# A mixer in another order: the decay chain ahead of the recurrent inputs, four of six gate projections among later products

## The chip, the cores and the metric

The kernel runs on one core of a Trainium2 chip, in one launch. The metric is the device time of that launch in microseconds. Three runs of the kernel before gave 1144.72, 1143.68 and 1144.16, a median of 1144.16. All times below are in microseconds (us) unless marked otherwise. TensorE (PE) multiplies matrices, VectorE (DVE) and ScalarE (ACT) do the elementwise work, GpSimd (POOL) does some, and SyncE (SP) issues most transfers.

## The reference

One layer of a hybrid decoder, in float32, over 256 prompt rows, 16 meta rows and 8 x 4 sample rows, 1024 wide. A layer norm, a mixer of three parallel branches behind one input projection and one output projection, a residual with layer norm, and a mixture of 32 experts, four for each row, with a layer norm behind it.

```python
# mixer, from the reference (cut)
xa, ga, vb, gb, q, k, v, rc, z = split(x @ w_in)
xc = conv4(xa)                       # branch a: recurrence
y_a = rglru(xc, ...) * gelu(ga)      # sigmoid gates from xc, a linear scan over time
uc = conv31(vb * sigmoid(gb))        # branch b: long convolution
y_b = silu(layer_norm(uc))
g = log_sigmoid(z @ w_gate2 + b_gate) / 16
o = gated_linear_attention(q, k, v, cumsum(g))   # branch c
y_c = rms_norm(o) * silu(rc)
y = concat(y_a, y_b, y_c) @ w_out
h = layer_norm(alpha * x + y)
out = layer_norm(alpha * h + moe(h))
```

The states of the three branches (the last inputs of both convolutions, the last hidden vector, the attention's matrix) are outputs too.

## The kernel before

The kernel is written engine by engine. Each engine has one list of instructions in a fixed order, and semaphores hold an instruction until what it needs is there. No scheduler changes this order.

TensorE's work in the mixer is a list of jobs (`JOBS`), one for each result in PSUM. A job writes bank (number of the job modulo 8), and it must wait until the job eight places earlier has been read out of that bank. The order of `JOBS` is thus both TensorE's order and the assignment of banks. `filled(eng, job)` waits until the job is in its bank, `copied(eng, job)` until it has been read.

The names of jobs: V0 to V2 values, VB and GB the long convolution's inputs and gates, XA0 to XA2 the recurrent inputs, K, Q and G keys, queries and decays, RG and IG the recurrence's two block gates (three each), GA0 to GA2 the gate projections of branch a, R0 to R2 those of branch c. KT and SC are transposed keys and scores of a chunk (0, 1 for the prompt, 2 for the samples), O outputs, STM and ST states, MU and VAR mean and variance of branch b, OA and OB state columns for output, W00 to W11 states of the samples, YC transposed outputs of branch c. P2 and P00 to P11 are the output projection, H and LG its normalised rows and the router's logits, POS the routing.

What the prediction's steps touch, with lines of the kernel before:

- The decay chain: G is added a bias (DVE L1048), ScalarE takes the softplus (L702 to L706), VectorE scans (L1053), ScalarE takes exponentials (L731 to L741), VectorE multiplies queries and keys (L1077 to L1092). The scores (L1544) wait for `qk_decayed`.
- The recurrence: short convolutions of XA on VectorE (L997 to L1001), RG and IG (PE L1433), their sigmoids (ACT L716), tanh and exponentials (L748, L751), products (DVE L1095 to L1102), a root (ACT L753) and the scan (DVE L1109). Its result times the Gelu of GA is `ya` (L1175).
- The long convolution: 31 taps for each of two parts on VectorE (L978 to L987). Their calls `taps(m, k0, k1)` are spread among the other work.
- The residual rows: the first layer norm's rows times gain and plus shift (DVE L1028, L1032), needed by the layer norm behind the mixer.
- The late part: MU, the square (ACT L802), VAR, a root, the reciprocal (DVE L1215), Silu (ACT L815); P2 (PE L1651) waits for `ya`, YC2 and, in its last columns, `yb`.

The window weights and the output weights lie in a ring of eight slots of 2 MB, in which branch data lie too. The same slots take the expert weights, each as soon as its last user is through (`load_first`, and then `load_group` with `w_used`). The expert loop on TensorE (L1730 to L1798) begins behind the routing and reads two experts at a time.

Two lines say how a job waits for its bank:

```python
if n >= 8:
    copied(pe, JOBS[n - 8])
emit(bk(name)).then_inc(bank_full, 1)
```

## Time and profile before

| | |
|---|---|
| median of three runs | 1144.16 |
| lowest, highest | 1143.68, 1144.72 |
| profiled execution, its own time | 1143.22 |
| its span | 1141.5 |
| PE busy | 1090.2 (96%) |
| DVE busy | 350.5 (31%) |
| ACT busy | 158.5 (14%) |
| HBM read | 423.38 MB, 373 GB/s over the span |

The mixer and the routing fill the span to about 207, and the expert loop the rest. Of a busy share over the whole span the expert loop makes up most; what the change is worth is read in the first 207 us and at the joint between both parts. A row of the timeline gives start and length of a merged group, engine, line and operation, what it writes and reads, and a count; a bracket behind it says how long the engine was idle before it and what released it. Matmul counts in the trace are twice those of the program, since a float32 product has two records here.

### The profile page before, as it was taken

What the parts mean: (1) busy time and instruction counts of PE and PEld (TensorE: products, weight loads), DVE (VectorE), ACT (ScalarE), POOL (GpSimd) and SP (SyncE); (2) the same over time, 40 slices, a digit from 0 to 9 for tenths busy, and PEclk for the clock granted to TensorE, in tenths of its full rate; (3) what the DMA queues carried; (4) which work ended last, traced back from release to release, by engine and by line L of the source; (5) the groups of instructions that cost most, each with busy time, mean ns of one, the idle gap of its engine ahead of it and who ended that gap; (6) DMA issues with size and microseconds to landing.
All of it is one profiled execution on the core that took longest, in us unless ns stands there. A gap on an engine that the chain in (4) does not pass through costs nothing.

```text
span 1141.5 us, 13868 instructions
## 1 busy us (share of the span) xinstructions
PE 1090.2 (96%) x5441; PEld 477.7 (42%) x5441; DVE 350.5 (31%) x831; ACT 158.5 (14%) x306; POOL 41.4 (4%) x101
## 2 busy tenths in 40 slices
PE   6998889999999999999999999999999999999996
PEld 4766535543434343434343433333434343434342
DVE  4956355322221313131313121212131212212134
ACT  3044342200101010101010101010101010100002
POOL 8000040000000000000000000000000000000000
PEclk9998788899999999999999999999999999999998
DMA  9631654699999999999999999999999999999992
GB/s 290 198 138 45 266 203 178 238 409 428 427 428 428 428 428 429 428 429 428 429 429 428 428 429 428 428 429 429 428 429 429 428 428 427 429 429 427 428 430 100
DMA packets 41094, 425.63 MB, mean 373 GB/s; under 512 B 6073, under 2 KB 12606, under 8 KB 16489
## 3 DMA queue, kind: packets, MB, share of 16 engines
q1 hardware_dynamic: 39185, 423.61, 88.9%
q0 software_dynamic: 1888, 1.75, 0.6%
q8 instruction: 12, 0.20, 0.1%
q14 instruction: 9, 0.07, 0.0%
HBM read 423.38 MB, written 2.17 MB: 373 GB/s over the span
## 4 chain that ended last, share of the span: by engine, by line
PE 73%; DMA 20%; DVE 3%; ACT 3%; issue 0%; SPq 0%; DVEq 0%; ACTq 0%
PE bank L1773 33%; DMA ring<-in_moe_w_dram 20%; PE bank L1788 11%; PE bank L1433 8%; PE bank L1730 7%; PE bank L1743 5%; PE bank L1686 2%; PE bank L1460 1%; PE bank L1798 1%; PE bank L1738 1%; PE bank L1438 1%; ACT ring L775 0%; DMA xt<-in_x_prompt_dram 0%; PE bank L1830 0%; PE bank L1576 0%; ACT ring L811 0%
## 5 line engine op out<-in xcount | busy, mean ns | idle before, releaser
L1773 PE MATMUL bank<-ring,hT 128*64 128x512 f32 x2048 | 454.7, 595 | 16.5 <-DMA ring<-in_moe_w_dram 15.9
L1773 PEld LDWEIGHTS bank<-ring,hT 128*64 128x64 f32 x2048 | 141.7, 137 | 301.2 <-issue 275.9
L1788 PE MATMUL bank<-ring 128*64 128x512 f32 x1024 | 226.8, 595 | 0.0
L1788 PEld LDWEIGHTS bank<-ring 128*64 128x64 f32 x1024 | 70.7, 137 | 132.6 <-issue 126.3
L1331 DVE TENSOR_SCALAR ring<-bank 128x512 f32<-128x512 f32 x32 | 22.1, 692 | 322.1 <-PE bank L1773 322.1
L1730 PEld LDWEIGHTS bank<-ring 128*128 128x128 f32 x792 | 92.8, 195 | 26.3 <-issue 26.0
L1730 PE MATMUL bank<-ring 128*128 128x128 f32 x792 | 99.1, 283 | 0.2 <-DVE ring L1278 0.2
L1348 DVE COPY ring<-bank 64x512 f32<-64x512 f32 x32 | 22.2, 694 | 230.1 <-PE bank L1788 230.1
L871 ACT ACTIVATE ring<-ring 128x512 f32<-128x512 f32 x32 | 20.1, 629 | 394.3 <-DVE ring L1331 394.3
L1284 DVE COPY hT<-bank 128x512 f32<-128x512 f32 x33 | 22.7, 688 | 138.7 <-PE bank L1730 138.7
L1743 PE MATMUL bank<-ring 128*128 128x512 f32 x128 | 63.5, 618 | 0.0
L1433 PE MATMUL bank<-hT,ring 128*128 128x304 f32 (+1 forms) x208 | 56.5, 434 | 0.0
L875 ACT ACTIVATE ring<-bank 128x512 f32<-128x512 f32 x32 | 19.1, 597 | 248.4 <-PE bank L1798 248.4
L1433 PEld LDWEIGHTS bank<-hT,ring 128*128 128x128 f32 x208 | 41.5, 201 | 14.0 <-issue 0.5
L1295 DVE TENSOR_TENSOR xt<-xt,bank 128x512 f32<-128x512 f32 x64 | 43.9, 686 | 5.8 <-PE bank L1743 5.5
L886 ACT ACTIVATE ring<-bank 64x512 f32<-64x512 f32 x32 | 18.9, 589 | 148.4 <-PE bank L1788 148.4
L1433 PE MATMUL bank<-ring 128*128 128x512 f32 (+1 forms) x92 | 36.8, 559 | 0.0
L1743 PEld LDWEIGHTS bank<-ring 128*128 128x128 f32 x128 | 21.7, 189 | 34.9 <-issue 34.9
L1686 PE MATMUL bank<-ring 32*64 32x512 f32 x264 | 35.9, 613 | 0.0
L639 POOL TENSOR_TENSOR ring<-ring 128x256 f32<-128x256 f32 x1 | 0.7, 722 | 964.3 <-ACT ring L903 964.3
L1798 PEld LDWEIGHTS bank<-ident,ring 128*128 128x128 f32 x128 | 18.0, 210 | 26.0 <-issue 26.0
L1433 PEld LDWEIGHTS bank<-ring 128*128 128x128 f32 x92 | 17.8, 196 | 18.2 <-issue 16.5
(301 smaller groups left out, 622.3 us busy)
## 6 DMA issues: line engine op xcount, KB each, us to landing
ring<-in_moe_w_dram SPq DMA_DIRECT2D x192, 2048.0 KB, 29.3
ring<-in_w_in_dram SPq DMA_DIRECT2D x5, 1536.0 KB, 13.0
ring<-in_w_out_dram SPq DMA_DIRECT2D x2, 2048.0 KB, 8.7
ring<-in_w_in_dram SPq DMA_DIRECT2D x1, 2048.0 KB, 14.8
lnbc<-in_ln_g_dram SPq DMA_DIRECT2D x3, 512.0 KB, 5.5
lnbc<-in_ln_b_dram SPq DMA_DIRECT2D x3, 512.0 KB, 10.1
xt<-in_x_prompt_dram SPq DMA_DIRECT2D x2, 512.0 KB, 4.3
ring<-in_state_gla_dram POOLq DMA_DIRECT2D x4, 144.0 KB, 7.0
```

The source lines that it names most:

```text
L871: act.activation(sg[:, :], g1[:, :], ACT.Sigmoid, scale=SALPHA).then_inc(sg_ready, 1)
L1284: dve.tensor_copy(xT[:, parity, 4 * b:4 * b + 4, :], bank[(2, 5)[b]][:, :].rearrange("p (k c) -> p k c", c=2 * CAP)).then_inc(xT_ready, 1)
L1295: dve.tensor_tensor(dst, dst, bank[COMB_BANK[c]][:, :], ALU.add).then_inc(y_added, 1)
L1331: dve.tensor_scalar(g1[:, :], bank[0][:, :], LIMIT, None, ALU.min).then_inc(g1_ready, 1)
L1348: dve.tensor_copy(eout[64 * j:64 * j + 64, 1, :], bank[OUT_BANK[j]][64:128, :]).then_inc(out_ready, 1)
L1433: ins = pe.matmul(out, a, b, start=n == 0, stop=n == len(pairs) - 1)
L1686: pe.matmul(bank[b][64 * h:64 * h + 64, :], bsel[e0:e0 + NE, j, :], b1_sb[e0:e0 + NE, h, :], start=True, stop=False)
L1730: ins = pe.matmul(out, xh[:, t, k * P:(k + 1) * P], pick[:, t, :], start=t == 0, stop=t == 2)
L1743: pe.matmul(out[:, :], putT[:, t * P:(t + 1) * P], eout[:, h, :], start=True, stop=True).then_inc(comb_full, 1)
L1773: ins = pe.matmul(bank[b][64 * h:64 * h + 64, :], xT[:, q, k, j * CAP:(j + 1) * CAP], ring[:, c:c + 512], start=False, stop=k == KT - 1)
L1788: ins = pe.matmul(bank[OUT_BANK[j]][64 * h:64 * h + 64, :], actT[:, j, k % 4, (k // 4) * CAP:(k // 4 + 1) * CAP], ring[:, c:c + 512], star ...
L1798: ins = pe.transpose(bank[3][:, k * P:(k + 1) * P], l1[:, k:512:4], ident[:, :])
```

## The change

It is one edit in many places, all of the same kind: instructions change their order, and with them the job table.

- `JOBS`: K, G and Q come ahead of XA. RG and IG go behind the first scores, R0 behind IG. GA2 goes behind ST1. VAR goes ahead of OA and OB, and YC1 ahead of P2.
- SP: the second input tile loads ahead of two small rows; qk loads ahead of xa; the two rows for the residual load last; the expert weights of slots 0 and 1 (`load_first(0)`) and 2 and 3 (`load_first(1)`) no longer stand behind the ln1 rows.
- ScalarE: XA's copies among the exponentials; values by sequence ahead of the sigmoids; GA is copied raw, and one Gelu over all three parts follows GA2 (`gelu_ready`); R is copied raw, and one Silu over all follows the root for branch b; the decays of the sample states come before that root; OA and OB behind the last Silu.
- VectorE: the long convolution's first part is cut into three pieces; the short convolutions come one by one around the products with decays; the recurrence and `ya` come behind the scores; the residual rows come around VAR.
- POOL: the stores of the recurrent and convolution states ahead of those of the matrix states.

```diff
-        "XA0", "XA1", "XA2", "K1", "K0", "G0", "G1", "Q0", "Q1", "RG0", "RG1", "RG2", "IG0", "IG1", "IG2", "V2",
-        "GA0", "GA1", "GA2", "KT2", "SC2e", "SC2o", "KT0", "SC0e", "SC0o", "R0", "STM", "KT1", "O0e", "O0o", "ST0",
...
+        "K1", "K0", "G0", "G1", "Q0", "Q1", "XA0", "XA1", "XA2", "V2", "GA0", "GA1", "KT2", "SC2e", "SC2o", "KT0", "SC0e", "SC0o",
+        "RG0", "RG1", "RG2", "STM", "KT1", "IG0", "IG1", "IG2", "R0", "O0e", "O0o", "ST0", "SC1e", "SC1o", "R1",
+        "O2q", "O2s", "O1e", "O1o", "ST1", "GA2", "MU", "R2", "VAR", "OA", "OB", "W00", "W01",
...
@@ SP
-            filled(sp, "V2")
+            filled(sp, "O2q")
             sp.wait_ge(h_ready, 1)
+            sp.wait_ge(outcols_ready, 2)
+            load_first(0)
+            filled(sp, "R2")
             filled(sp, "GA2")
             sp.wait_ge(ya_ready, MA)
-            sp.wait_ge(outcols_ready, 2)
+            load_first(1)
             sp.wait_ge(h0_ready, 3)
             sp.dma_start(lnbc[:, 0, :], ln1_g.to_broadcast([P, D])).then_inc(ld_ln, 16)
             sp.dma_start(lnbc[:, 1, :], ln1_b.to_broadcast([P, D])).then_inc(ld_ln, 16)
-            filled(sp, "O2q")
-            load_first(0)
-            filled(sp, "R2")
-            load_first(1)
@@ ScalarE
+            def gate_a(m):
+                filled(act, f"GA{m}")
+                st.do(act.activation(yT[:, m, 0:TOUT], bk(f"GA{m}")[:, 0:TOUT], ACT.Copy), read_of(f"GA{m}"))
+
+            gate_a(0)
+            gate_a(1)
+            st.settle()
+            act.wait_ge(consts_ready, 4)
+            values_by_sequence(0)
...
-            silu_r(2)
+            act.wait_ge(o_root_in, 1)
+            st.do(act.activation(rsq[:, :, :], rsq[:, :, :], ACT.Sqrt), o_root)
+            gate_a(2)
             st.settle()
...
+            st.do(act.activation(yT[:, 0:MA, :], yT[:, 0:MA, :], ACT.Gelu_apprx_tanh), gelu_ready)
+            decayed_states(0)
             copied(act, "MU")
             st.do(act.activation(sgb[:, :, 0:TOUT], uc[:, :, :], ACT.Square), sq_ready)
...
+            decayed_states(1)
+            gate_c(2)
             copied(act, "VAR")
             st.do(act.activation(brst[:, :], brst[:, :], ACT.Sqrt), b_root)
...
+            st.settle()
+            st.then(act.activation(rT[:, :, :], rT[:, :, :], ACT.Silu))
@@ VectorE
-            for m in range(MA):
-                short_conv(m)
...
             st.then(dve.tensor_tensor(kc[:, :, :], k_sb[:, :, 0:TOUT], E[1][:, :, 0:TOUT], ALU.mult), exp_used)
+            dve.wait_ge(colA_moved, 1)
+            short_conv(0)
...
+            short_conv(1)
+            short_conv(2)
...
+            taps(1, 24, WB)
+            dve.wait_ge(o_root, 1)
+            st.then(dve.reciprocal(rsq[:, :, :], rsq[:, :, :]))
+            finish_outputs(2)
+            finish_outputs(0)
+            finish_outputs(1)
+            dve.wait_ge(gelu_ready, 1)
+            for m in range(MA):
+                st.do(dve.tensor_tensor(yT[:, m, 0:TOUT], yT[:, m, 0:TOUT], xc[:, m, META:], ALU.mult), ya_ready)
+            state_out("ST1", 1)
             filled(dve, "MU")
...
+            residual_rows(0)
             filled(dve, "VAR")
...
+            residual_rows(1)
             dve.wait_ge(b_root, 1)
@@ TensorE
             scores_jobs(2)
             keys_job(0)
             scores_jobs(0)
-            pe.wait_ge(ld_win["r"], 16)
-            project("R0", "r", 0, P, TOUT)
+            pe.wait_ge(xc_ready, MA)
+            pe.wait_ge(ld_wbd, 16 * 20)
+            block_gates(0, "RG")
             copied(pe, "V2")
             state_job("STM", 2, SAMP, T2)
             keys_job(1)
+            block_gates(1, "IG")
+            pe.wait_ge(ld_win["r"], 16)
+            project("R0", "r", 0, P, TOUT)
```

TensorE's order from the queries to the first output product. In the kernel before (L1460 with 288 columns: Q; the next row: RG and IG; L1522: V2; L1433 128x288 x24: GA0 to GA2; L1438: transposed keys; L1544: scores; L1575: the first output product):

```order
L1460 MATMUL bank<-hT,ring 64x288 x32
L1433 MATMUL bank<-ring 128x304 x14
L1522 MATMUL bank<-ring,hT 48x192 x16
L1433 MATMUL bank<-hT,ring 128x288 x24
L1438 MATMUL bank<-ident,ring 48x128 x2
L1544 MATMUL bank<-ring 32x32 x4
L1438 MATMUL bank<-ident,ring 128x128 x2
L1544 MATMUL bank<-ring 128x128 x4
L1433 MATMUL bank<-hT,ring 128x288 x8
L1586 MATMUL bank<-ring 64x96 x4
L1438 MATMUL bank<-ident,ring 128x128 x2
L1575 MATMUL bank<-ring 128x96
```

And in the changed kernel, from its Q (now L1469) to its scores and gates (lines moved by 9, L1552 are scores):

```order
L1469 MATMUL bank<-hT,ring 64x288 x32
L1442 MATMUL bank<-hT,ring 128x304 x24
L1525 MATMUL bank<-ring,hT 48x192 x16
L1442 MATMUL bank<-hT,ring 128x288 x16
L1447 MATMUL bank<-ident,ring 48x128 x2
L1552 MATMUL bank<-ring 32x32 x4
L1447 MATMUL bank<-ident,ring 128x128 x2
L1552 MATMUL bank<-ring 128x128 x4
L1442 MATMUL bank<-ring 128x304 x7
L1594 MATMUL bank<-ring 64x96 x4
L1442 MATMUL bank<-ring 128x304 x7
L1442 MATMUL bank<-hT,ring 128x288 x8
```

XA's three (x24) stand behind Q, two of the three GA ahead of the scores, and the fourteen products of RG and IG and the eight of R0 ahead of the output products.

VectorE's order around the variance. Before (L1155: normalised outputs; L1140: ST1; L1211: VAR; L1161: YC2 and YC0; L1215, L1216: reciprocal and product of branch b):

```order
L1155 TENSOR_TENSOR ring<-ring 128x384
L1140 SCALAR_TENSOR_TENSOR ring<-ring,bank 128x96 x2
L1211 TENSOR_SCALAR ring<-bank 128x288
L1161 TENSOR_TENSOR ring<-bank,ring 128x3x32
L1161 TENSOR_TENSOR ring<-bank,ring 128x3x128
L1215 RECIPROCAL ring<-ring 128x288
L1216 TENSOR_TENSOR ring<-ring 128x576
```

In the changed kernel (L1144: normalised outputs; L1209: `ya`; L1129: ST1; L1213: MU; L1037 and L1035: the residual rows; L1219: VAR; L1222, L1223: reciprocal and product; L1150: YC2):

```order
L1144 TENSOR_TENSOR ring<-ring 128x384 x2
L1209 TENSOR_TENSOR ring<-ring 128x288 x3
L1129 SCALAR_TENSOR_TENSOR ring<-ring,bank 128x96 x2
L1213 SCALAR_TENSOR_TENSOR ring<-bank,ring 128x288 x2
L1037 TENSOR_TENSOR xt<-xt,lnbc 128x1024 x2
L1219 TENSOR_SCALAR ring<-bank 128x288
L1035 TENSOR_TENSOR xt<-xt,lnbc 128x1024 x2
L1222 RECIPROCAL ring<-ring 128x288
L1223 TENSOR_TENSOR ring<-ring 128x576
L1150 TENSOR_TENSOR ring<-bank,ring 128x3x32
```

The products of `ya`, MU and the six residual instructions (four of them of the full size, shown) have come between the normalised outputs and the transposed ones that P2 waits for.

## Rows read from the trace of the kernel before

**Rows 1.** The page's chain that ended last, by engine.
```profile
PE 73%; DMA 20%; DVE 3%; ACT 3%; issue 0%; SPq 0%; DVEq 0%; ACTq 0%
```

**Rows 2.** The chain in order of time (start, length, what), its first long transfer.
```profile
684.95 32.13 DMA ring<-in_moe_w_dram
```

**Rows 3.** Windows at the joint: length, busy (x instructions) of five engines, PEclk, DMA.
```profile
204.00:206.00 2.00, 2.00 (x12) 2.00 (x11) 0.62 (x6) 1.26 (x2) 0.00 (x0) 0.52 0.00 0
...
210.00:212.00 2.00, 2.00 (x12) 0.70 (x10) 0.00 (x0) 0.00 (x0) 0.00 (x0) 1.00 0.00 0
212.00:214.00 2.00, 2.00 (x16) 1.19 (x13) 0.00 (x0) 0.00 (x0) 0.00 (x0) 1.00 0.93 229
```

**Rows 4.** The timeline of TensorE in the mixer, start and length first.
```profile
72.05 7.43 PE L1433 MATMUL bank<-ring 128*128 128x304 f32 x28
...
82.15 11.91 PE L1433 MATMUL bank<-hT,ring 128*128 128x288 f32 x48
93.90 0.38 PE L1438 MATMUL bank<-ident,ring 128*48 128x128 f32 x2
...
97.68 0.71 PE L1544 MATMUL bank<-ring 48*128 48x128 f32 x4 [2.14 <-ACT ring L757]
...
106.28 0.43 PE L1575 MATMUL bank<-ring 128*128 128x96 f32 x2 [2.38 <-DVE ring L1138]
...
113.12 6.13 PE L1433 MATMUL bank<-hT,ring 128*128 128x288 f32 x16
...
125.76 2.29 PE L1433 MATMUL bank<-ring,ones 128*128 128x288 f32 x4
...
138.04 2.82 PE L1596 MATMUL bank<-ring 32*64 32x384 f32 x8 [4.13 <-ACT ring L775]
...
144.61 4.38 PE L1651 MATMUL bank<-ring 128*32 128x256 f32 x48
...
153.57 1.76 PE L1596 MATMUL bank<-ring 32*64 32x384 f32 x8 [1.21 <-ACT ring L775]
155.26 15.40 PE L1433 MATMUL bank<-ring 128*128 128x512 f32 x32
...
172.43 14.00 PE L1433 MATMUL bank<-ring 128*128 128x512 f32 x32
```

**Rows 5.** Windows of the mixer, columns as in rows 3 (PEclk third from the end).
```profile
106.00:108.00 2.00, 1.72 (x7) 1.32 (x8) 0.52 (x3) 0.00 (x0) 0.00 (x0) 0.73 0.73 262
...
114.00:116.00 2.00, 2.00 (x5) 1.43 (x5) 1.97 (x6) 0.00 (x0) 0.00 (x0) 0.50 0.00 0
116.00:118.00 2.00, 2.00 (x7) 1.41 (x7) 1.52 (x3) 0.00 (x0) 0.00 (x0) 0.71 0.00 0
...
124.00:126.00 2.00, 2.00 (x13) 1.43 (x13) 0.00 (x0) 0.33 (x1) 0.00 (x0) 0.50 0.97 418
```

**Rows 6.** The timeline of VectorE.
```profile
26.93 3.49 DVE L1028 TENSOR_TENSOR xt<-xt,lnbc 128x1024 f32<-128x1024 f32 x3 [0.71 <-DMA lnbc<-in_ln_b_dram]
...
39.55 11.56 DVE L984 SCALAR_TENSOR_TENSOR ring<-ring 128x256 f32<-128x256 f32 x29
...
64.03 0.98 DVE L1048 TENSOR_SCALAR ring<-bank,ring 128x304 f32<-128x304 f32 x2
...
89.67 0.79 DVE L1092 TENSOR_TENSOR ring<-ring 128x608 f32<-128x608 f32 x1 [0.20 <-ACT ring L733]
...
99.24 2.06 DVE L1109 TENSOR_TENSOR_SCAN ring<-ring 128x912 f32<-128x912 f32 x1
...
145.19 1.94 DVE L1215 RECIPROCAL ring<-ring 128x288 f32<-128x288 f32 x1
```

**Rows 7.** The timeline of ScalarE.
```profile
82.96 1.28 ACT L731 ACT_TABLE_LOAD   x1
84.26 1.28 ACT L731 ACTIVATE ring<-ring 128x128 f32<-128x128 f32 x4
...
91.19 1.43 ACT L751 ACTIVATE ring<-ring 128x304 f32<-128x304 f32 x3
```

More of the change, by code:

```diff
@@ L611, in _ @@
             pool.dma_start(o_conv_b_s[0, :, 0:WB - 1 - DSEQ, :], state_conv_b[0, :, DSEQ:WB - 1, :]).then_inc(st_out, 16)
-            copied(pool, "ST1")
-            copied(pool, "W11")
-            for h in range(NH):
-                b, p = head(h)
-                pool.dma_start(o_gla_p[0, 0, h, :, :], Sp[b:b + DK, p, :]).then_inc(st_out, 16)
-                pool.dma_start(o_gla_s[0, :, h, :, :].rearrange("s d e -> d s e"), S0[b:b + DK, p, :, :]).then_inc(st_out, 16)
             copied(pool, "OA")
@@ L627, in _ @@
                 pool.dma_start(o_conv_b_s[0, n, WB - 1 - DSEQ:WB - 1, :], packOB[r:r + DSEQ, :]).then_inc(st_out, 16)
+            copied(pool, "ST1")
+            copied(pool, "W11")
+            for h in range(NH):
+                b, p = head(h)
+                pool.dma_start(o_gla_p[0, 0, h, :, :], Sp[b:b + DK, p, :]).then_inc(st_out, 16)
+                pool.dma_start(o_gla_s[0, :, h, :, :].rearrange("s d e -> d s e"), S0[b:b + DK, p, :, :]).then_inc(st_out, 16)
             pool.wait_ge(st_out, 16 * ST_OUT)
@@ L816, in _ @@
                                      bias=colB[:, m, WB + 2:WB + 3]), yb_ready)
+            for job, dst, n, w in (("OA", packOA, 36, DA), ("OB", packOB, 62, DB)):
+                filled(act, job)
+                st.do(act.activation(dst, bk(job)[0:n, 0:w], ACT.Copy), read_of(job))
             filled(act, "W01")
@@ L1037, in _ @@
             sample_taps(0)
-            taps(0, 0, WB)
-            dve.wait_ge(colA_moved, 1)
-            for m in range(MA):
-                short_conv(m)
+            taps(0, 0, 10)
             glu(1)
             sample_taps(1)
+            taps(0, 10, 18)
             dve.wait_ge(ld_gate, 16 * 5)
@@ L1171, in sample_state_out @@
                           read_of(job))
-            for m in range(MA):
-                copied(dve, f"GA{m}")
-                st.do(dve.tensor_tensor(yT[:, m, 0:TOUT], yT[:, m, 0:TOUT], xc[:, m, META:], ALU.mult), ya_ready)
             keys_out(2)
@@ L1180, in _ @@
             scores_out(0)
-            taps(1, 22, 26)
+            taps(1, 8, 14)
             state_out("STM", None)
             keys_out(1)
+            taps(1, 14, 20)
+            copied(dve, "IG2")
+            st.do(dve.tensor_tensor(iu[:, :, :], iu[:, :, :], xc[:, :, :], ALU.mult))
+            taps(1, 20, 24)
+            dve.wait_ge(a_ready, MA)
+            st.then(dve.tensor_tensor(xc[:, :, :], ra[:, :, :], ra[:, :, :], ALU.mult))
+            st.then(dve.scalar_tensor_tensor(tsq[:, :, :], xc[:, :, :], 1.0, tsq[:, :, :], ALU.add, ALU.mult), rg_root_in)
             dve.wait_ge(eg_ready, 1)
@@ L1193, in _ @@
             mean_squares(2)
-            st.then(dve.tensor_scalar(rsq[:, 0::2, :], rsq[:, 0::2, :], 1.0 / DV, EPS, ALU.mult, ALU.add), o_root_in)
+            copied(dve, "O1o")
+            mean_squares(1)
+            st.then(dve.tensor_scalar(rsq[:, :, :], rsq[:, :, :], 1.0 / DV, EPS, ALU.mult, ALU.add), o_root_in)
+            taps(1, 24, WB)
[5 more added lines that the diff above has]
+            dve.wait_ge(gelu_ready, 1)
+            for m in range(MA):
+                st.do(dve.tensor_tensor(yT[:, m, 0:TOUT], yT[:, m, 0:TOUT], xc[:, m, META:], ALU.mult), ya_ready)
+            state_out("ST1", 1)
             filled(dve, "MU")
@@ L1493, in _ @@
                 project(f"GB{m}", "vbgb", DB + m * P, P, TALL)
-            pe.wait_ge(ld_win["xa"], 16)
-            for m in range(MA):
-                project(f"XA{m}", "xa", m * P, P, TALL)
             pe.wait_ge(ld_win["qk"], 32)
@@ L1526, in _, with block_gates @@
             pe.wait_ge(ld_win["ga"], 16)
-            for m in range(MA):
-                project(f"GA{m}", "ga", m * P, P, TOUT)
+            project("GA0", "ga", 0, P, TOUT)
+            project("GA1", "ga", P, P, TOUT)
+            def block_gates(g, name):
+                for m in range(MA):
+                    ks = [k for k in range(MA) if abs(k - m) <= 1]
+                    job(f"{name}{m}", lambda b: chain(b[:, 0:TALL], [(wbd[:, g, k, m * P:(m + 1) * P], xc[:, k, :]) for k in ks]))
             cols0 = [cols[0], cols[1], (2 * P, TALL)]
@@ L1627, in _ @@
             state_job("ST1", 1, 0, P)
+            project("GA2", "ga", 2 * P, P, TOUT)
             pe.wait_ge(uc_ready, MB)
@@ L1630, in _ @@
             project("R2", "r", 2 * P, P, TOUT)
+            pe.wait_ge(sq_ready, 1)
+            job("VAR", lambda b: chain(b[:, 0:TOUT], [(ones[:, :], sgb[:, m, 0:TOUT]) for m in range(MB)]))
             pe.wait_ge(outcols_ready, 2)
@@ L1634, in _ @@
             sample_state_jobs(0)
-            pe.wait_ge(sq_ready, 1)
-            job("VAR", lambda b: chain(b[:, 0:TOUT], [(ones[:, :], sgb[:, m, 0:TOUT]) for m in range(MB)]))
             y_c_job(2, 1)
             y_c_job(0, 2)
+            y_c_job(1, 3)
             pe.wait_ge(ya_ready, MA)
```

173 lines of the change are left out of this document (69 added, 104 removed), and 3 rows, old and new, of the table JOBS.

## The prediction

> **What bounds the kernel now.** I read the page's chain first, then its last part in order of time, then the matmuls of the mixer in order of time with their idle brackets, and the granted clock in short stretches beside them. TensorE holds 73% of the chain, the expert weights' transfers 20% [rows 1]. In order of time these transfers end the chain only from 684.95 on [rows 2]. That late part would keep its length whatever the mixer did, so the question is what its stream of transfers hangs on. Before it, the ring is full and the DMA engines stand still: share 0.00 at 204 and again at 210, then 0.93 from 212 [rows 3]. The refill waits for TensorE to use the first expert piece. A mixer that ends earlier by some time therefore moves the refill, and the whole kernel, by the same time. This is the premise of all that follows.
>
> In the mixer TensorE is the chain up to the scores at 93.90. Then it waits: 2.14 before 97.68, 2.38 before 106.28, 4.13 before 138.04, 1.21 before 153.57 [rows 4]. Waiting is only half of it. In the stretches at 114 and 124 the granted clock is 0.50, the lower of its two levels, 1.2 GHz; it had fallen at 106 to 108, behind the idle time before 106.28, and it came back in 116 to 118 while the long projection at 113.12 ran [rows 4, 5]. That projection took 6.13, where three of its kind took 11.91 at full clock, 3.97 each [rows 4]. At 124 it was low a second time with no idle bracket ahead of it; small 96-column products had run since the projection ended at 119.25.
>
> **Step 1: from the projections to the scores.** The change takes the six block-gate products (7.43 at 72.05) and one of three gate projections (GA2, 3.97) from ahead of the scores [rows 4]; the rest only changes places, XA behind Q among it. TensorE had no idle time on this stretch. So the scores would start at 93.90 - 7.4 - 3.9 = 82.6, if the decayed keys are there. Before, they took from the bias add at 64.03 to the last product at 89.67 + 0.79 = 90.46, that is 26.4 [rows 4, 6]. XA ahead of this chain (three projections of 304 columns, 4.1 each by 3.97 for 288) is gone, so the add moves to about 52 and the keys are ready by 78.4 even with the old ScalarE waits for gate products in them. One short convolution now stands inside (2.8, an estimate: eight instructions of the size of a tap): 81.2. Without those waits I walk it to about 71. Either is ahead of 82.6, so VectorE and ScalarE cover this step. The other two convolutions end about 77, against 85 when the recurrent gates want them.
>
> The loads: the two 512 KB broadcasts for the residual go behind the window weights and qk ahead of xa, so qk has 2.5 MB less ahead of it; xa, later in the queue, is wanted 17 us later than the qk weights. Cost nothing. Moving the second input tile ahead of two small rows may give up to 0.8 at the start; I take nothing.
>
> **Step 2: from the scores to the first output product.** Before: 93.90 to 106.28, 12.4 with waits of 2.14 and 2.38 in it. Now the recurrent gates, 7.4, and R0 (3.9) lie there with the same small products, dense: scores 2.3, RG 3.7, state and keys 0.8, IG 3.7, R0 3.9. So 82.6 + 14.4 = 97.0 against 106.28. The banks these products take are read in time: the sigmoid of the first is done about 88, and its bank is wanted at 93. What was hidden work of VectorE (the short convolutions) stays hidden; the recurrence, formerly ahead of the scores, moves behind them.
>
> **Step 3: the new late chain.** The recurrence now goes by: last sigmoid 93.6, three tanh 1.43, a table load 1.28, three exponentials 1.43 [rows 7], so 97.8. Then VectorE without a break: two products of 1.1, state and scores 1.3, mean squares 1.15, a product and small ones 1.8, the scan 2.06 [rows 6], sample outputs 0.6, two more mean squares 2.3, and the last seven taps with the sum (0.40 each, 11.56 for 29) [rows 6], 3.3. That is 115.6 if O1 is there by 110.6. (Sizes of VectorE and ScalarE without a row of their own are estimates by their columns from rows 6 and 7.) TensorE's side: O0 to ST1 is 19.5 before (106.28 to 125.76) [rows 4], over half of it at the low clock [rows 5]; at full clock throughout I count 13.9, an estimate (R1 3.97 for 6.13, the small products about 9.9 for 13.4). GA2, now behind it, takes 3.97 or, at low clock first, 5.7. So the convolution sum is ready at 115.6 to 117.1, GA2 at 115.0 to 118.3.
>
> Then in turn: GA2 copied 0.4, table load 1.28, one Gelu of 864 columns 0.95: 117.7 to 121.0. VectorE's three ya products 1.2, ST1 0.5, MU 0.8; then **the residual multiplies, 3.49** [rows 6], formerly at 26.93 when VectorE had nothing else, VAR 0.5, **the residual adds**, again 3.5, the reciprocal 1.94 [rows 6], a product 0.8 and the transposed sample outputs 0.3. That is 13.1, so P2 starts at **130.8 to 134.1**; it started at 144.61 [rows 4]. TensorE idles 4 to 7 there, as YC1, its last work before, ends at 125.6 to 129.3. The residual rows are the dearest move: 7.0 that had cover and now have half at most (the variance product hides behind the first). The old wait of 4.13 for ScalarE's copies by sequence goes, since they are made before the sigmoids. Next late after it is this wait for VectorE.
>
> **Step 4: P2 to the logits.** Before, P2 to the first long product took 144.61 to 155.26 = 10.65, with waits for the last Silu and for the copies. Now the last Silu is done 1.1 after the normalised rows, and the second set of copies (2.85, behind OA and OB) about 4.5 after P2 starts. P2 begins behind idle time, at low clock, and earns the full one: 5.2 plus 1.8 for the state products = 7.0; all at low clock, 8.7. The two long products behind took 15.40 at 155.26 and 14.00 at 172.43 [rows 4], so 0 to 1.4 more. From there nothing differs: LN1, routing and the experts run as they did. POOL's stores of recurrent and conv states pass ahead of the matrix states; the same 22 transfers end before its four clears, which had over 15 us of room. The SP queue asks for the expert weights of slots 0 and 1 earlier and of 2 and 3 at about 121 to 124; the two ln1 rows behind them land about 137 to 141, and LN1 needs them only by the logits at 152.
>
> **The sum.** Least: 10.5 + 2.0 + 0 = 12.5. Most: 13.8 + 3.7 + 1.4 = 18.9. I take 12.2 + 3.4 + 1.2 = **16.8**, nearer to the most, because the rows show that a long projection brings the clock back. The profiled execution is 1143.22 with a span of 1141.5; that is 0.9 below the median of 1144.16. So 1126.4 for a profiled one and **1127.4** as a median.
>
> **A rule against it.** The Gelu's table load stands on this late chain. The load at 82.96 has no idle bracket before it and the next activation starts at 84.26, 1.28 + 0.02 later [rows 7]; I use 1.28. The Trainium skill (ScalarE: Activation LUTs, What ACT_TABLE_LOAD costs) puts a drain of about 1.38 beside the load, 2.66 for a switch; by that the Gelu would be later by 1.4 and the sum 15.4 in place of 16.8. The trace disagrees, and I give it 2 in 100, inside the forecast's own.
>
> **The rivals.**
> *A. A longer late wait (20%).* Every VectorE step from the recurrence on is now serial. If 5 us more come together ahead of P2 (ScalarE's sixteen state decays and the last Silu run also share that stretch), the gain is 12 or less: 1129.5 to 1134. For it: VectorE stood idle in much of 105 to 140 before, and this order has given that room away. Against: each duration is from a row.
> *B. The weights' stream sets the end anyway (3%).* Then the time is 1144. For: DMA share stays full for 900 us, and transfers end the chain. Against: share 0.00 up to 212 [rows 3].
> *C. The lower clock stays, slower than before (3%).* The mechanism is in rows 5: small products at 82.6 to 84.9, then a clock that does not come back before P2. RG, IG, R0, R1 and GA2 would cost twice (3.7, 3.7, 3.97, 3.97, 3.97 = 19.3 more), the small products about 4 more. That is 23 against a gain of 16.8: 1150.5. It decides from 17 us of added low clock on. Against: the projection at 113.12 raised it, and five such blocks lie on this stretch.
> *D. The keys are not ready at 82.6 (4%).* If the chain kept its old place, at 90.5, TensorE would wait 8 with the clock falling: gain 5 to 8, 1136 to 1139. Against: the bound of step 1.
> My forecast, 12.5 to 18.9 with one to two either side: 70%.
>
> **Numbers.** The range is 1122.5 to 1133.5: the sum's ends (1125.3 to 1131.7), 0.8 of the start and luck with the clock below, most of rival A above. A measurement of this kernel tells 0.2%, 2.3 us, from no change. Faster 0.94 (forecast, A and D), same 0.03 (B), slower 0.03 (C).
>
> **What would show it.** Right: no idle bracket on TensorE up to the first output product, which starts at about 97; the scores at about 82.6; one idle time of 4 to 7 us before P2's first product, released by VectorE; the refill starting at about 195 in place of 212. Wrong: an idle time before the scores (step 1), a clock of 0.50 in most of 85 to 115 (C), a late part whose end does not move with the refill (B), or P2 later than 136 (A).

## The result and the profile after

The changed kernel takes 1125.42 us as the median of four runs (1124.08 to 1126.09); the kernel before took 1143.92 beside it (four runs, 1136.83 to 1144.72). The ratio is 0.985, 95% interval 0.981 to 0.989: faster by 1.1 to 1.9%. Beside the later experiments the kernel before ran 32 times more; over all 36 runs its median is 1143.2, its range 1134.97 to 1146.78. The forecast was 1127.4, its range 1122.5 to 1133.5. The profiled execution of after is 1125.65 with a span of 1123.9, to set beside 1143.22 and 1141.5.

The page of after, busy times and the chain by engine:
```profile
PE 1079.3 (96%) x5441; PEld 472.3 (42%) x5441; DVE 349.4 (31%) x829; ACT 160.2 (14%) x307; POOL 40.8 (4%) x101
...
PE 72%; DMA 23%; DVE 3%; ACT 1%; issue 0%; SPq 0%; DVEq 0%
```
TensorE does the same 5441 matmuls in 1079.3, 10.9 less than the 1090.2 of before. A reordering removes no product; products at the lower clock are what can become shorter. In the chain ACT falls from 3% [rows 1] to 1%, and the transfers hold 23% for 20%.

TensorE in the mixer, in order of time (start, length, what it is, idle bracket), the rows that answer to [rows 4]:
```profile
82.03 0.38 PE L1447 MATMUL bank<-ident,ring 128*48 128x128 f32 x2
...
83.61 3.85 PE L1442 MATMUL bank<-ring 128*128 128x304 f32 x14
...
88.14 3.75 PE L1442 MATMUL bank<-ring 128*128 128x304 f32 x14
...
95.61 0.36 PE L1583 MATMUL bank<-ring 128*128 128x96 f32 x2
...
100.04 5.50 PE L1442 MATMUL bank<-hT,ring 128*128 128x288 f32 x16
...
111.32 4.15 PE L1442 MATMUL bank<-hT,ring 128*128 128x288 f32 x16
116.14 1.24 PE L1442 MATMUL bank<-ring,ones 128*128 128x288 f32 x4 [0.68 <-DVE ring L992]
...
130.80 4.98 PE L1665 MATMUL bank<-ring 128*32 128x256 f32 x64 [5.15 <-DVE ring L1150]
...
137.15 14.00 PE L1442 MATMUL bank<-ring 128*128 128x512 f32 x32
...
152.92 14.00 PE L1442 MATMUL bank<-ring 128*128 128x512 f32 x32
...
188.63 5.37 PE L1786 MATMUL bank<-ring,hT 128*64 128x512 f32 x24 [0.28 <-DVE hT L1293]
```
82.03 are the scores, 83.61 and 88.14 the recurrent gates with 3.85 and 3.75, 95.61 the first output product, 130.80 P2, 188.63 the first product of the expert loop. From the first projection at 11.79 up to 116 no bracket stands; then 0.68, and one of 5.15 before P2, released by VectorE. The kernel before had brackets of 2.14, 0.53, 2.38, 4.13, 0.27, 1.82 and 1.21 between its scores and its long products: 12.48 against 5.83.

The granted clock (columns as in rows 3, PEclk third from the end), to set beside [rows 5]:
```profile
98.00:100.00 2.00, 2.00 (x20) 1.51 (x20) 1.60 (x3) 1.25 (x2) 0.00 (x0) 0.85 0.00 0
...
126.00:128.00 2.00, 0.00 (x0) 0.00 (x0) 2.00 (x3) 1.96 (x3) 0.00 (x0) 0.68 1.03 442
...
130.00:132.00 2.00, 1.20 (x12) 0.69 (x16) 2.00 (x6) 1.59 (x4) 0.00 (x0) 0.50 0.94 401
132.00:134.00 2.00, 2.00 (x28) 1.19 (x24) 0.40 (x1) 2.00 (x7) 1.78 (x4) 0.62 0.91 340
...
192.00:194.00 2.00, 2.00 (x11) 0.50 (x7) 0.00 (x0) 0.00 (x0) 0.00 (x0) 1.00 0.63 131
```
The clock fell at 98 to 100, at 1.00 until then and with no idle bracket ahead, among small products of 96 and 128 columns; R1 at 100.04, half of it at 0.50, took 5.50 where GA2 at 111.32 took 4.15. It fell again within the wait before P2 and came back at 132 to 134. Summed over windows of 2 us between 92 and 166 as 2 x (1 - PEclk), the clock cost at most 5.1 us here and 15.3 before (at most, because a low clock in a wait costs nothing). The last row is the refill: it begins at 192 to 194 where it began at 212 [rows 3].

VectorE ahead of P2, to set beside [rows 6]:
```profile
82.52 0.42 DVE L1104 COPY ring<-bank 48x256 f32<-48x256 f32 x1 [6.73 <-PE bank L1447]
...
111.38 0.56 DVE L1137 TENSOR_TENSOR ring<-ring 128x384 f32<-128x384 f32 x1 [1.49 <-ACT ring L779]
...
115.66 0.42 DVE L992 TENSOR_TENSOR ring<-ring 128x256 f32<-128x256 f32 x1
...
118.18 1.20 DVE L1209 TENSOR_TENSOR ring<-ring 128x288 f32<-128x288 f32 x3 [0.31 <-ACT ring L803]
...
120.47 3.48 DVE L1037 TENSOR_TENSOR xt<-xt,lnbc 128x1024 f32<-128x1024 f32 x3
...
124.25 3.48 DVE L1035 TENSOR_TENSOR xt<-xt,lnbc 128x1024 f32<-128x1024 f32 x3
127.65 1.94 DVE L1222 RECIPROCAL ring<-ring 128x288 f32<-128x288 f32 x1
...
130.30 1.18 DVE L1150 TENSOR_TENSOR ring<-bank,ring 128x96 f32<-128x96 f32 x3
```
It stands idle for 6.73 before the scores. The 1.49 before 111.38 is a wait for ScalarE's copy of the last output pair. From 111.38 to P2 it is busy but for 0.31. The two groups of residual rows of 3.48 are in this chain.

ScalarE there, to set beside [rows 7]:
```profile
110.94 0.33 ACT L779 ACTIVATE ring<-bank 128x192 f32<-128x192 f32 x1 [1.23 <-PE bank L1584]
...
115.93 1.28 ACT L803 ACT_TABLE_LOAD   x1
117.22 0.92 ACT L803 ACTIVATE ring<-ring 128x864 f32<-128x864 f32 x1
```
The copy at 110.94 waits for TensorE's last output product, and VectorE at 111.38 for the copy: TensorE's outputs, and not the recurrence, set when the last taps of the long convolution start. The table load takes 1.28, and the Gelu starts 0.01 behind it.

**Where the 17.6 us came from.** The first long product behind P2 starts at 137.15 for 155.26, 18.1 earlier. Of this 0.8 is gained at the start (the projections of VB and GB begin at 25.06 for 25.88), 6.7 are waits (12.48 - 5.83), and the remaining 10.6 are the same products in less time. That is the clock, all but a few tenths: leaving out the waits, the windows up to the long product give 13.3 us lost to the lower clock before and 3.1 after, 10.2 apart. Then the two long products give 1.4 (14.00 for 15.40). In the routing stage 0.6 is lost, again with the clock (2 x (1 - PEclk) from 166 to 208 is 8.5 for 6.8). So the expert loop starts 18.9 earlier (188.63 for 207.53). Behind it 1.3 is lost: in the 20 us from 24.4 after the loop's start the transfers move 390 GB/s for 403. The span ends 17.6 earlier. The 1.3 is this execution's and not the order's: in the profiles of e1 to e7 the part behind the loop's start takes 933.8 to 934.5, as before (934.0), and only here 935.3.

### The profile page after: what moved, and what is told of

Its sections match the earlier page's. It is cut to its first block, busy times and chain, and to the rows that moved or that the text cites. A ratio compares the mean times of both kernels' runs of the same rounds, so it can differ in the third digit from the quotient of the medians.

```text
span 1123.9 us, 13864 instructions
## 1 busy us (share of the span) xinstructions
PE 1079.3 (96%) x5441; PEld 472.3 (42%) x5441; DVE 349.4 (31%) x829; ACT 160.2 (14%) x307; POOL 40.8 (4%) x101
## 3 DMA queue, kind: packets, MB, share of 16 engines
q0 software_dynamic: 1888, 1.75, 0.6%
## 4 chain that ended last, share of the span: by engine, by line
PE 72%; DMA 23%; DVE 3%; ACT 1%; issue 0%; SPq 0%; DVEq 0%
PE bank L1786 32%; DMA ring<-in_moe_w_dram 23%; PE bank L1801 10%; PE bank L1442 9%; PE bank L1743 7%; PE bank L1756 5%; PE bank L1699 2%; PE bank L1469 1%; PE bank L1811 1%; PE bank L1751 1%; PE bank L1447 1%; PE bank L1665 0%; PE bank L1689 0%; PE bank L1843 0%; DVE xt L1035 0%
## 5 line engine op out<-in xcount | busy, mean ns | idle before, releaser
L891 ACT ACTIVATE ring<-bank 64x512 f32<-64x512 f32 x32 | 18.9, 589 | 148.4 <-PE bank L1801 148.4
## 6 DMA issues: line engine op xcount, KB each, us to landing
ring<-in_w_in_dram SPq DMA_DIRECT2D x5, 1536.0 KB, 13.3
ring<-in_w_in_dram SPq DMA_DIRECT2D x1, 2048.0 KB, 13.3
```

## The experiments

All variants of the changed kernel start from it, those of the kernel before from that. The variants of the changed kernel are compared with each other and with it by their medians of four to seven runs, since each spreads over 1.5 to 4 us and the kernel before over 12. They ran in three batches, and the changed kernel itself only ahead of them; e1, e2 and e5 overlap its range (1124.08 to 1126.09), so by the times alone these three are not told from it. Intervals are of the ratio to the kernel before, whose medians beside these batches were 1140.33 (e1 to e4), 1142.25 (e5 to e8) and 1143.54 (e9 to e12).

**e1: the third gate projection back ahead of the scores.**
```diff
             project("GA1", "ga", P, P, TOUT)
+            project("GA2", "ga", 2 * P, P, TOUT)
...
             state_job("ST1", 1, 0, P)
-            project("GA2", "ga", 2 * P, P, TOUT)
```


> The changed kernel with one part undone: GA2 again directly behind GA1, ahead of the scores (and ScalarE's copy of it beside the other two). My theory: TensorE is dense up to the first output product, so GA2's 3.9 us push the scores from 82.0 to 86.0 and the last output pair by as much; VectorE's chain behind it moves along, the convolution sum from 116.1 to about 120, and P2 starts at 134.5 to 135 in place of 130.8. About 4 us slower than the changed kernel, 1129.5. Rival (a product may stand anywhere on a dense TensorE, only the sum counts): P2 at 130.8, 1125.5.


Measured 1127.06 (1125.71 to 1127.70), ratio 0.983 to 0.993. TensorE:
```profile
98.58 0.36 PE L1583 MATMUL bank<-ring 128*128 128x96 f32 x2
...
102.72 4.15 PE L1441 MATMUL bank<-hT,ring 128*128 128x288 f32 x16
...
117.47 2.29 PE L1441 MATMUL bank<-ring,ones 128*128 128x288 f32 x4 [4.75 <-DVE ring L991]
...
132.43 4.91 PE L1664 MATMUL bank<-ring 128*32 128x256 f32 x64 [3.88 <-DVE ring L1149]
```
VectorE:
```profile
112.70 0.56 DVE L1136 TENSOR_TENSOR ring<-ring 128x384 f32<-128x384 f32 x1 [1.49 <-ACT ring L780]
```
The first output product is 3.0 later, 98.58: GA2's 3.9, less 0.9 by which this execution is ahead at the start (24.14 for 25.06). VectorE moves along as expected, its first copy behind the scores from 82.52 to 85.49 and its scan from 103.77 to 106.47. The last output pair is only 1.3 later (112.70 for 111.38 on VectorE), because here the clock did not fall before it: R1 took 4.15 for 5.50. MU then waits 4.75 for the convolution sum, where GA2 had stood, and P2 is 1.6 later. So GA2 behind the outputs fills a hole that is there anyway, and this execution hid 2.5 us of its price by luck with start and clock. The medians differ by 1.6, where about 4 was expected; in the pair e2 and e3, which differ by the same move, they differ by 4.4. The price lies between, and these runs do not fix it.

**e2: gate products ahead of the scores, GA2 left.**
```diff
+            block_gates(0, "RG")
+            block_gates(1, "IG")
             cols0 = [cols[0], cols[1], (2 * P, TALL)]
```
and out of their places behind the scores.


> The changed kernel with RG and IG again ahead of the scores, GA2 left late. My theory: the recurrent inputs are ready at about 76, the six products fit densely behind GA1 at 82 (scores at 89.4), and the same products are dense either way up to the first output product at 95.6; the late chain is held by the last output pair, which stays where it is. P2 at 130.8 within 0.5, time within 1 us of the changed kernel: moving the block gates behind the scores is worth nothing by itself. Rival (the recurrence behind the scores is what gains): 3 to 7 us slower, with an idle time on TensorE before the scores or the outputs.


Measured 1124.36 (1123.66 to 1125.13), 0.980 to 0.991. Scores at 88.14, first output product at 94.35 (95.61 in after), P2 at 131.13 with the same bracket of 5.15. TensorE, then VectorE:
```profile
109.13 6.66 PE L1442 MATMUL bank<-hT,ring 128*128 128x288 f32 x16
```
```profile
118.50 1.20 DVE L1209 TENSOR_TENSOR ring<-ring 128x288 f32<-128x288 f32 x3 [2.94 <-ACT ring L803]
```
P2 and the time (1.1 under after) are about as expected, the way to them is not. The last output pair did not stay where it was: the convolution sum begins at 113.35 for 115.66 (1.1 of it from the start, 24.00 for 25.06). Then the clock fell, GA2 took 6.66 for 4.15, and VectorE waited 2.94 for the Gelu behind it. That the block gates' place is worth nothing is what the times say; that it would be so with the clock up is not shown.

**e3: both.**


> The changed kernel with RG, IG and GA2 all ahead of the scores: of the projections' order only the decay chain ahead of the recurrent inputs is left. My theory: the sum of both parts, P2 at 134.5 to 135, about 1129.5; then the decay chain's move together with the late order carries some 10 of the first 14 us. Rival: the two parts add to more than 4 us.


Measured 1128.72 (1127.44 to 1129.68), 0.984 to 0.994; P2 at 134.48, and it took 6.46 at the lower clock for 4.98. As expected, but not the plain sum of both parts (3.3 for 1.6 and -1.1). Its mixer has more of the lower clock (2 x (1 - PEclk) from 92 to 166 is 8.5 for 5.1), so part of the 3.3 is the clock's.

**e4: XA ahead of the decay chain.**
```diff
+            pe.wait_ge(ld_win["xa"], 16)
+            for m in range(MA):
+                project(f"XA{m}", "xa", m * P, P, TALL)
```
moved ahead of K, G and Q, and with it xa's load on the queue and its copies on ScalarE.


> The changed kernel with XA again ahead of K, G and Q (ScalarE's copies and the load order of xa and qk too), VectorE's order as in the changed kernel. My theory: from the bias add of G to the last decayed key the changed kernel takes 19.5 us (50.75 to 70.25). With G 12.3 later the keys are there at 82.6, half a microsecond behind TensorE, but the last short convolution ends at about 88 in place of 76, where RG wants it at 84: one wait of 3.5 to 4.5, and the recurrence and P2 later by as much, 134.5 to 135.5, 1129 to 1130. Rival (the old kernel's place of the keys): the keys at 90, wait of 8, the clock falls and 8 to 12 us are lost.


Measured 1131.11 (1129.93 to 1131.97), 0.989 to 0.994. TensorE:
```profile
81.90 0.40 PE L1446 MATMUL bank<-ident,ring 128*48 128x128 f32 x2 [0.73 <-DVE ring L1096]
...
87.44 5.68 PE L1441 MATMUL bank<-ring 128*128 128x304 f32 x14 [3.87 <-DVE ring L1005]
```
Both waits are the expected ones: the keys hold the scores for 0.73, and RG waits 3.87 for the last short convolution (L1005). Not expected was the clock: RG then ran at the lower level, 5.68 for 3.85, and P2 starts at 136.61, 1.1 behind the latest start expected. The decay chain ahead of XA is worth 5.7 us (1131.11 for 1125.42), the most of the moves undone here.

These four undo half of the gain, if the parts add: 3.3 for the gates (e3), 5.7 for the decay chain (e4), some 9 of 18. The other half was not undone by itself. Among it are the copies by sequence ahead of the sigmoids (the wait of 4.13 before W00 is gone), the one Silu of R and YC1 ahead of P2 (those of 1.82 and 1.21 are gone) and the clock behind these waits. The rows show the waits gone; what each move is worth is not shown.

**e5: the residual rows in VectorE's idle time ahead of the scores.**
```diff
+            dve.wait_ge(ld_ln, 32)
+            dve.wait_ge(xhat_ready, 3)
+            residual_rows(0)
+            residual_rows(1)
```
and out of the late chain.


> The changed kernel with the six residual instructions (7.0 us) put behind the third short convolution on VectorE, into its 6.7 us of idle time before the scores. My theory: VectorE's part of the late chain loses the 7.0, but ScalarE's root for branch b is not ready before 125.4 (state decays, R2's copy and a table load stand ahead of it), so the reciprocal starts at about 125.5 in place of 127.65 and P2 at 128.7 in place of 130.8: 2 us. The scores' copies may be 0.3 later and cost nothing. 1123.5. Rival (VectorE alone sets the late wait): P2 at 125.7, right behind YC1, 5 us gained, 1120.5.


Measured 1123.67 (1122.54 to 1124.91), 0.981 to 0.987; P2 at 129.77, 1.1 later than expected. VectorE:
```profile
122.50 0.46 DVE L1220 TENSOR_SCALAR ring<-bank 128x288 f32<-128x288 f32 x1 [2.04 <-PE bank L1442]
125.37 1.95 DVE L1222 RECIPROCAL ring<-ring 128x288 f32<-128x288 f32 x1 [2.42 <-ACT ring L810]
...
129.10 1.19 DVE L1154 TENSOR_TENSOR ring<-bank,ring 128x96 f32<-128x96 f32 x3 [0.98 <-ACT ring L814]
```
Of the 7.0 taken out 1.0 arrives at P2. The rest turns into waits, 5.4 in all: for TensorE's variance product (2.04), for ScalarE's root (2.42) and for its scaled Silu (0.98). In after ScalarE was only a little ahead of VectorE: the root was done at 125.44 and used at 127.65, the scaled Silu done at 129.09 and used at 130.30. The dearest move, as the prediction called it, was dear by 1 us at P2 and 1.75 in the median.

**e6: e5, and on ScalarE the second state decays behind the copies.** `decayed_states(1)` moves down, so that ScalarE's root comes sooner.


> The kernel of the run before with ScalarE's order changed too: the second eight state decays go from ahead of the root of branch b to behind the second set of copies by sequence (VectorE then waits for each half of the decays apart). My theory: the root comes 2 us earlier, about 123.4, and then the scaled Silu of R (ready about 127.5) holds the transposed outputs: P2 at 127.8, and its idle time is short enough that the clock stays, P2 4.3 in place of 4.98. First long product at about 133.7 in place of 137.15: 3.5 us faster than the changed kernel, 1122. Rival: nothing beyond the run before.


Measured 1122.00 (1120.23 to 1122.68), 0.979 to 0.985. P2 at 127.75 as expected, but it took 6.36 where 4.3 was expected. The clock was at 0.50 when it began and came back only at 132 to 134, near P2's end at 134.1. The wait is shorter (2.16), the price of its clock is higher.

**e7: nine filler products ahead of P2 in the changed kernel.** They write a bank that is free until P2, and nobody reads them.
```diff
+                for _ in range(count):
+                    pe.matmul(bk(name)[:, 0:TALL], ones[:, :], hT[:, 0, :], start=True, stop=True)
+            filler("P2", 9)
```


> The changed kernel with nine products of ones with hT (304 columns, 4.4 us at full clock) into P2's own bank in the idle time before P2; they are overwritten. My theory: the clock stays at the upper level over the wait, P2 takes 4.3 in place of 4.98 and W10 and W11 as before: 0.6 to 0.7 us gained, 1124.8. Rival (the clock costs nothing here): P2 4.98 again, no change.


Measured 1122.90 (1119.81 to 1123.65), 0.979 to 0.986. TensorE:
```profile
125.25 4.77 PE L1453 MATMUL bank<-hT,ones 128*128 128x304 f32 x18
130.56 3.66 PE L1671 MATMUL bank<-ring 128*32 128x256 f32 x64 [0.54 <-DVE ring L1150]
...
136.20 14.00 PE L1442 MATMUL bank<-ring 128*128 128x512 f32 x32
```
P2 takes 3.66 for 4.98, and the clock is 1.00 throughout there. From P2 to the long product are 5.64 for 6.35, so the fillers gain 0.7, as expected; that bears out the mechanism at this wait: what it costs behind its own length is the clock. The median is lower by 2.5, more than expected. Most of that is not the fillers': in the profile 1.2 more is gained between the long product and the loop, where 2 x (1 - PEclk) sums to 6.8 for 8.5, as in e2 to e6 without fillers, and 1.0 behind the loop's start.

**e8: the same in three waits of the kernel before** (4 ahead of O0, 7 ahead of W00, 2 ahead of W10).


> The kernel before with fillers of the same kind in three of its waits on TensorE: four before the first output product, seven before W00, two before W10. No wait gets shorter and nothing moves; only the clock can change. My theory: about half of the change's gain was the clock, so it stays up at 106 and 138 and 4 to 7 us are gained against the kernel before (1137 to 1140), less than the clock's full share because it falls at 124 without idle time anyway. Rival (the gain was the idle time alone): within 1 us of the kernel before.


Median 1142.07 of 11 runs (1135.07 to 1142.84), ratio 0.998 to 1.002: a miss. The profiled run was the fastest of all. So it was profiled again, and so was the kernel before, whose own times spread over 12 us:


> The kernel before with filler products in three of its waits, profiled once more; the first profile was of a run at 1135.07, 7 us under the median. Theory (the fillers do not reliably keep the clock; that one run was a lucky one): a profile at 1141 to 1142 shows the same short waits and some 20 us of the mixer at 0.50. Rival (the fillers do keep the clock in the mixer and something else costs 7 us): the mixer is at 1.00 nearly throughout, the expert loop starts at about 199.5, and the rest is longer.

> The kernel before, unchanged, profiled once more, since its times spread over 11 us (1135 to 1147) while those of the changed kernel spread over 2. Theory (its spread is the granted clock of the mixer, which falls or does not fall behind each of its waits): order of the work, length of the waits and everything from the routing stage on read as in the first profile; what differs is how many microseconds of the mixer are at 0.50, and the time differs by about half of that. Rival (the spread comes from the expert weights' transfers): the expert loop starts at 207.5 as before and the part behind it has another length.


They took 1142.33 and 1146.08. The kernel with fillers, first the run profiled in e8, in the mixer (columns as in rows 3):
```profile
96.00:108.00 12.00, 9.74 (x49) 7.02 (x49) 9.93 (x25) 3.94 (x7) 2.30 (x7) 1.00 0.33 90
108.00:114.00 6.00, 6.00 (x32) 4.59 (x32) 3.66 (x10) 0.38 (x2) 0.00 (x0) 0.72 0.09 33
122.00:130.00 8.00, 8.00 (x36) 6.18 (x36) 2.01 (x5) 3.03 (x8) 0.00 (x0) 1.00 1.00 399
134.00:142.00 8.00, 5.36 (x56) 2.63 (x54) 6.25 (x13) 5.17 (x21) 0.00 (x0) 0.79 0.71 303
```
The other, windows and then three rows of TensorE (the group of four fillers in the first wait is 107.21):
```profile
96.00:108.00 12.00, 9.86 (x38) 7.10 (x39) 11.21 (x28) 4.60 (x7) 2.31 (x7) 0.72 0.21 59
122.00:130.00 8.00, 8.00 (x28) 5.85 (x27) 2.12 (x6) 0.33 (x1) 0.00 (x0) 0.57 1.03 440
142.00:154.00 12.00, 9.83 (x80) 5.23 (x82) 5.01 (x7) 9.77 (x28) 0.00 (x0) 0.72 0.42 154
```
```profile
99.85 6.68 PE L1433 MATMUL bank<-hT,ring 128*128 128x288 f32 x16
...
107.21 2.21 PE L1444 MATMUL bank<-hT,ones 128*128 128x304 f32 x8
109.26 0.36 PE L1580 MATMUL bank<-ring 128*128 128x96 f32 x2
```
The program is the same. In one the clock falls twice in the mixer (at 110 and at 137), in the other from 98 on, ahead of the first filler, and three times more. A product ahead of the wait then takes longer (R0 6.68 for 4.15), the wait is over before the fillers are, and they hold up the real work: the last copy that the output product needs is done at 107.5, and it starts at 109.26, with no idle bracket. What that does over seven profiled executions ("low": the sum of 2 x (1 - PEclk) from 92 to 166; "rest": span less start of the expert loop):

| | low | loop starts | rest | time |
|---|---|---|---|---|
| e9, before | 17.0 | 210.16 | 934.1 | 1146.08 |
| before | 15.3 | 207.53 | 934.0 | 1143.22 |
| e10, before and fillers | 10.2 | 205.57 | 934.9 | 1142.33 |
| e8, before and fillers | 3.4 | 199.45 | 933.8 | 1135.07 |
| e11, before and second tile first | 10.2 | 199.41 | 934.2 | 1135.37 |
| after | 5.1 | 188.63 | 935.3 | 1125.65 |
| e12, below | 3.4 | 182.54 | 934.1 | 1118.32 |

The rest stays within 1.5 us while the loop's start moves by 28: the theory of e9 holds, the transfers are not the spread. e10's 10.2 are 20 us at 0.50, as its theory said. The clock's sum alone does not order the rows, though: e10 and e11 have the same 10.2 and lie 6.2 apart. Of this 1.6 is the start (26.90 and 25.26), and the rest is what e10's fillers hold up and where the low stretches lie: one ahead of a wait is hidden by it (e11 runs low from 96 to 104, and the wait before its first output product is 0.27 for 2.38).

That fillers reliably save time in the kernel before is refuted. Over all runs they did raise the mean granted clock, 0.981 to 0.988 for 0.973 to 0.983, with the same median time: a clock kept up within a wait is no gain by itself.

**e11: of the change only the place of the second input tile.**
```diff
+            sp.dma_start(xt[:, 1, :], x_prompt[0, P:2 * P, :]).then_inc(ld_x[1], 16)
```
ahead of the two small rows instead of behind them.


> Of the change only the place of the second input tile's load, ahead of the two small rows. Theory (an entry in the queue of transfers costs its place; the first projection waits for this tile): in the profile the second normalisation and the first long projection start 0.8 to 1.0 us earlier (11.8 in place of 12.75). In the time this is under what one look can tell. Rival (the first projection hangs on the weights): no shift.


TensorE at the start:
```profile
6.40 0.26 PE L1438 MATMUL bank<-ident,ring 16*128 16x16 f32 x1 [6.40 <-DMA ring<-in_ln_b_dram]
...
11.98 6.48 PE L1433 MATMUL bank<-ring,hT 128*128 128x384 f32 x16
```
The first projection starts at 11.98, in the two profiles of before at 12.75 and 13.21: 0.8 to 1.2, about as expected, although the small rows' product is later (6.40 for 4.47). All ten profiles with the second tile first have it at 11.79 to 11.98, the four without (e8 and e10 too) at 12.75 to 13.29. The run's own 1135.37 is the luck of its clock, as the table shows: low 10.2, and part of that ahead of a wait.

**e12: the pieces that did something, together.** e5, e6, e2, and four fillers each ahead of P2 and ahead of H1a.


> The changed kernel with the three pieces that did something put together: residual rows in VectorE's idle time ahead of the scores, the second state decays on ScalarE behind the copies, gate products ahead of the scores, and four filler products each ahead of the first normalised product (P2) and ahead of the first product on the transposed second norm (H1a). Theory (two costs are left, a wait of 2 us and the clock that falls in it): P2 starts at 127.8 and takes 3.7 to 4.3 in place of 6.36, the long product starts at 133, and the time is 1118 to 1120.5. Rival (fillers are worth nothing behind a wait of 2 us, the clock falls in the small products anyway): P2 takes over 5.5, the time is 1121 to 1123, as without fillers. A second rival: the fillers delay what they stand ahead of, and it is above 1123.


Measured 1118.32 (five runs, 1117.88 to 1121.27), ratio 0.976 to 0.981, faster than the kernel before, and below the whole range of after, by some 7 us in the median. Of this 1.1 is ahead at the start already in the profile (23.94 for 25.06). TensorE:
```profile
109.20 6.53 PE L1443 MATMUL bank<-hT,ring 128*128 128x288 f32 x16
...
125.75 2.21 PE L1454 MATMUL bank<-hT,ones 128*128 128x304 f32 x8
128.07 3.66 PE L1672 MATMUL bank<-ring 128*32 128x256 f32 x64
...
133.38 7.13 PE L1443 MATMUL bank<-ring 128*128 128x512 f32 x16
```
P2 at 128.07 takes 3.66, the long product starts at 133.38: the theory's numbers, the rival's are out. Against e6 P2 and the state products take 5.31 for 7.73 up to the long product, 2.4 less; P2 itself starts 0.3 later, and the long product 2.1 earlier. From there to the loop it is 49.16 for 50.75, 1.6 less with the second filler, where the clock's sum falls from 6.8 to 3.4. GA2 at 109.20 took 6.53: here, too, the clock fell without a wait ahead of it.

## Why the prediction was right

**Premise: the refill moves with the mixer.** Right. The transfers end the chain from 610.08 on in after and not from 684.95 [rows 2], yet the span follows the loop's start, 17.6 for 18.9; the table shows it over 28 us. Rival B is out. The 1.3 between was no term of the sum.

**Step 1.** Scores at 82.03, forecast 82.6, no bracket. The keys were ready at 70.3 (the walk said 71, the bound 81.2), the convolutions at 75.8 (77). Rival D is out; e4 shows what it would have looked like. The start gave the 0.8 that I noted and did not take; e11 shows that this load's place gives it to the first projection. What arrives at 25 varies more, 23.94 to 25.26 in the ten profiles with the tile first, since the first projection took from 5.33 to 6.48.

**Step 2.** First output product at 95.61, forecast 97.0. The recurrent gates fit without a wait; 13.6 for 14.4.

**Step 3.** P2 at 130.80, the early end of 130.8 to 134.1, with one wait of 5.15 for VectorE. The convolution sum was ready at 116.1, the GA2 projection at 115.5, the Gelu at 118.1, all near the early ends. VectorE's late chain: 13.1 by forecast, 12.6 measured from the Gelu's `ya` to P2 (118.18 to 130.80). Three points of the reading were off. VectorE "without a break" from 97.8 comes by the listed durations to 112.5 and not to 115.6; the trace has breaks instead (1.56 before its first product on the exponentials, 2.36 before the sample outputs, 1.49 before the last mean squares), and TensorE's last output pair sets the sum. So 115.6 holds only through its condition, O1 there by 110.6 (it ended at 110.9). I placed "the dearest move" at 7.0 with half of it hidden; e5 shows that it costs 1 at P2, since ScalarE's root and Silu stand close behind it. And what the move of GA2 is worth, 3.9 in step 1, is not fixed: 1.6 by e1, 4.4 by e3 against e2.

**Step 4.** From P2 to the long product 6.35 where I took 7.0 (P2 4.98 for 5.2, the state products 1.4 for 1.8), against 10.65: 4.3 gained for 3.4. The pair of long products 14.00 and 14.00: 1.4 for 1.2.

**The sum.** Taken 12.2 + 3.4 + 1.2 = 16.8; measured 13.8 + 4.3 + 1.4 = 19.5, less 0.6 in the routing stage and 1.3 behind it = 17.6. Mis-sized are the first term, 13.8 in place of 12.2, and the second, 4.3, which lies above the most I gave it, 3.7. The losses that I had not counted brought the total back near the forecast, and the 1.3 among them is one execution's, so the hit is closer than the working deserves. The least, 12.5, and most, 18.9, were for the first three terms, and 19.5 lies above the most.

**What I had not asked.** A single run of before is a draw: its times go from 1135 to 1147, with mean granted clocks from 0.983 down to 0.973, and the profiles show the places where the clock falls to differ. I took the low clock in its one profile for a property of the order. Against its fastest execution (1134.97) the change is worth 9.5, against its slowest 21, against the median of its 36 runs 17.8.

**The table load.** It took 1.28 + 0.01 between neighbours again. By the Trainium skill (ScalarE: Activation LUTs, What ACT_TABLE_LOAD costs) the switch would be 2.66; the trace disagrees here too.

**Rivals.** A: P2 came at 130.80, so no 5 us came together; e4 shows such a case at 1131.11, inside A's range. C: the clock fell twice and came back both times; low 5.1 us, far from 17. What stays open is what makes it fall at 98 in one execution and later in another. That the changed kernel spreads over 2 us only, in its four runs, because it has fewer waits is argued, not shown.

## What to carry to other kernels

A wait on TensorE has two prices, its length and the lower clock behind it; here more than half of the gain in the two profiles (10.6 of 18.1) was the same products in less time, nearly all of it the clock, so count products beside each wait. Before a move of work on one engine is priced, ask who is close behind it: 7.0 us off VectorE's chain gave 1.0. Before the difference of two profiles is put down to an edit, take off what each gained by its start and its clock: 3.9 us put ahead of the scores seemed to cost 1.6 (e1), with 2.5 of luck in it. When a kernel's times spread over 1%, take a second profile of it before a difference is explained. Fillers pay only while they end before the wait does.

## What the runs showed of the hardware

- The clock fell without an idle bracket in front of it: at 98 to 100 in after, where TensorE had had none since 11.79, and at 106 to 108 in e12, both among dense float32 products of 96 and 128 columns. It stayed at 0.50 into the long projection behind them and came back at 102 to 104 in after.
- Filler products ahead of a wait's end kept it at 1.00 through 5 us of waiting (e7: P2 3.66 for 4.98). In the kernel before three sets of them moved the median by nothing (ratio 0.998 to 1.002): the clock fell elsewhere too, and fillers that ran past the end of the wait held up real work (e10, 107.5 to 109.26).
- Two executions of the same program differ by 6 us at the expert loop (e8 and e10: 199.45 and 205.57) with the same work in front of it; 1.3 of this stands at the start (25.62 and 26.90).
